# A two-block hybrid decoder: gate and up products token by token with 512 moving columns, product transposed on TensorE, three norms in token halves

## The reference, cut to what matters

```
def swiglu(h, w_gate, w_up, w_down):
    return (jax.nn.silu(h @ w_gate) * (h @ w_up)) @ w_down
...
    for l in range(DEPTH):
        x = x + 0.5 * swiglu(rms_norm(x, ffn1_norm[l]), ffn1_w_gate[l], ffn1_w_up[l], ffn1_w_down[l])
        h = rms_norm(x, mix_norm[l])
        mem_n = rms_norm(mem, mem_norm[l])
...
        x = x + 0.5 * swiglu(rms_norm(x, ffn2_norm[l]), ffn2_w_gate[l], ffn2_w_up[l], ffn2_w_down[l])
```

## Time and profile before

| | us |
|---|---|
| median of 3 runs | 1759.2 |
| the runs | 1759.13 to 1759.99 |
| the profiled execution | 1756.48, its span 1754.7 |

### The profile page before, as it was taken

How to read it: one execution, slowest core, us unless ns; L and a number is a source line. 1 busy time by engine, 2 the same in 40 slices (tenths; PEclk the granted TensorE clock), 3 DMA queues, 4 the chain that set the end, 5 groups by cost and what they waited for, 6 DMA issues and landing times.

```text
span 1754.7 us, 27203 instructions
## 1 busy us (share of the span) xinstructions
PE 1661.3 (95%) x11578; PEld 1531.1 (87%) x11578; DVE 1048.1 (60%) x1506; ACT 872.9 (50%) x1297; POOL 97.7 (6%) x72
## 2 busy tenths in 40 slices
PE   7999899999989899999888999999999998789999
PEld 7989777989977799999887899989999997679998
DVE  6875564896646555555786645455646465555554
ACT  4975363686445435435445533344454357443332
POOL 0112000012200000000240000000000000000000
PEclk9999999999999899999999999998999999899999
DMA  7624224552313465555321555544665553035552
GB/s 224 191 66 135 71 73 145 157 158 89 97 49 117 163 213 191 171 190 169 121 83 62 168 186 179 188 140 135 196 204 175 185 169 120 24 113 179 190 192 97
DMA packets 204297, 253.24 MB, mean 144 GB/s; under 512 B 17808, under 2 KB 183952, under 8 KB 204048
## 3 DMA queue, kind: packets, MB, share of 16 engines
q1 hardware_dynamic: 204176, 251.49, 44.9%
HBM read 250.43 MB, written 1.05 MB: 143 GB/s over the span
## 4 chain that ended last, share of the span: by engine, by line
PE 78%; DVE 8%; ACT 6%; issue 5%; DMA 1%; POOL 1%; SPq 0%; DVEq 0%; ACTq 0%; POOLq 0%
PE bank L784 77%; ACT arena L1377 4%; DVE weights_rest L1889 2%; ACT weights_high L1377 1%; PE bank L842 1%; DVE arena L2036 1%; DMA ring<-in_w_in 1%; ACT L1377 1%; ACT L1372 1%; DVE small L2206 0%; DVE x L2252 0%; DVE weights_rest_more L1889 0%; DVE arena L2224 0%; POOL arena L2520 0%; DMA vec<-in_vec 0%
## 5 line engine op out<-in xcount | busy, mean ns | idle before, releaser
L784 PE MATMUL bank<-xT_high,weights_high 128*128 128x256 f32 (+1 forms) x2352 | 676.1, 288 | 8.9 <-DVE weights_rest L1889 4.1
L784 PE MATMUL bank<-xT_rest,weights_high 128*128 128x256 f32 (+1 forms) x2352 | 658.3, 284 | 0.0
L784 PE MATMUL bank<-xT_high,weights_rest 128*128 128x256 f32 (+1 forms) x2048 | 581.4, 285 | 0.0
L1889 DVE TENSOR_TENSOR weights_rest<-ring,weights_high 128x1024 fp32r<-128x1024 f32 (+3 forms) x414 | 486.6, 1225 | 98.8 <-ACT weights_high L1377 95.1
L1377 ACT ACTIVATE weights_high<-ring 128x1024 fp32r<-128x1024 f32 (+3 forms) x414 | 400.6, 1019 | 253.9 <-PE bank L784 235.6
L784 PEld LDWEIGHTS bank<-xT_high,weights_high 128*128 128x128 f32 (+1 forms) x2352 | 454.2, 193 | 19.4 <-issue 8.9
L784 PEld LDWEIGHTS bank<-xT_rest,weights_high 128*128 128x128 f32 (+1 forms) x2352 | 448.1, 192 | 3.5 <-issue 2.0
L784 PEld LDWEIGHTS bank<-xT_high,weights_rest 128*128 128x128 f32 (+1 forms) x2048 | 395.7, 193 | 0.6
L1377 ACT ACTIVATE arena<-bank 128x512 f32<-128x512 f32 (+4 forms) x253 | 134.5, 547 | 390.3 <-PE bank L784 327.4
L784 PE MATMUL bank<-arena 128*128 128x128 f32 (+2 forms) x1416 | 209.4, 307 | 37.3 <-ACT arena L1377 22.9
L784 PEld LDWEIGHTS bank<-arena 128*128 128x128 f32 (+1 forms) x1416 | 180.2, 203 | 63.6 <-ACT arena L1377 22.6
(11 more groups left out here) (180 smaller groups left out, 1698.1 us busy)
## 6 DMA issues: line engine op xcount, KB each, us to landing
ring<-in_w_in SPq DMA_DIRECT2D x36, 1024.0 KB, 5.2
ring<-in_ffn_w_gate SPq DMA_DIRECT2D x36, 1024.0 KB, 5.4
ring<-in_ffn_w_up SPq DMA_DIRECT2D x35, 1024.0 KB, 5.4
ring<-in_ffn_w_down SPq DMA_DIRECT2D x34, 1024.0 KB, 4.9
ring<-in_w_out SPq DMA_DIRECT2D x22, 1024.0 KB, 4.9
ring<-in_w_in_a SPq DMA_DIRECT2D x11, 1024.0 KB, 5.2
ring_more<-in_ffn_w_down SPq DMA_DIRECT2D x10, 1024.0 KB, 5.1
ring_more<-in_ffn_w_up SPq DMA_DIRECT2D x9, 1024.0 KB, 5.3
```

The lines of the kernel that those rows point to most:

```text
L784: return eng.matmul(o, a, b, start=first, stop=last)
L1889: TTs(rest_slot(b)[:, part], raw_slot(b)[:, part], high_slot(key)[:, part].bitcast(F32), ALU.subtract).then_inc(*dv.mark(("rest", key, z)))
```

## The change

**Gate and up.** A weight block now holds four of the eight 128-row slices of both matrices, 256 gate columns beside 256 up columns. There are two such blocks a pair, (g, j, 0) and (g, j, 1), each landed by two transfers of 512 KB. `gate_up` holds 128 tokens of `xh` or `xl` stationary and moves 512 columns of weights: 48 matmuls of 512 columns a pair. Within a block the slices come in the order 2, 3, 0, 1, so the first matmul asks for both pieces of the block.

**The product** is made token-major in halves of 128 tokens by 256, then four transposes of a pair bring it back (`hidden_transposes`). ScalarE copies the high part out of the bank (`hidden_high`) and VectorE subtracts (`hidden_rest`); VectorE's cast goes.

**The norms** of f10, f20 and f21 run by token halves (`norm_by_tokens`, `add_and_norm`): the first half is added, scaled, transposed and multiplied in pair 0 before the second. `first_block` goes, `st_final` becomes a part of them. The last two down products are interleaved by token halves. ScalarE and VectorE split up to two blocks ahead of pair 0's SiLU, where it was three.

```diff
-                cols((st, "g", j), w[f"{n}_w_gate_2"][l], 256 * j, 256 * j + 256)
-                cols((st, "u", j), w[f"{n}_w_up_2"][l], 256 * j, 256 * j + 256)
+                for z in range(2):
...
+                    out.append(((st, "g", j, z), pieces, (4, 512)))
...
+            def gate_up(st, j, z, t, b, order):
...
+                for n, k in order:
+                    if j == 0 and id in BY_TOKENS.values():
+                        pe.wait_ge(*at(("xl", id, t, k)))
...
+                    if k % 4 >= 2:
+                        second_half(key)
+                    for i, (a, v) in enumerate(products(wv, [xh, xl])):
+                        ins = mm(b[:, 0:512], v[:, k, t * P:t * P + P], a[:, k % 4, :], n == 0 and i == 0, n == KD - 1 and i == 2)
...
+                    if j == 0 and id in BY_TOKENS.values():
+                        for z in range(2):
+                            gate_up(st, j, z, 0, b[0], order[4 * z:4 * z + 4])
+                        transposes(id, 1)
+                        for z in range(2):
+                            gate_up(st, j, z, 1, b[1], order[4 * z:4 * z + 4])
+                    else:
+                        for z in range(2):
+                            for t in range(NT):
+                                gate_up(st, j, z, t, b[t], order[4 * z:4 * z + 4])
+                            if j and z == 0:
+                                hidden_transposes(st, j - 1)
...
+                    if j and j < pairs - 1:
+                        down(st, j - 1, (0, 1), (0, 1), used=True)
+                if end == pairs:
+                    down(st, pairs - 2, (0,), (0, 1))
+                    hidden_transposes(st, pairs - 1)
+                    down(st, pairs - 2, (1,), (0,))
+                    down(st, pairs - 1, (0,), (0, 1))
+                    down(st, pairs - 2, (1,), (1,), used=True)
+                    down(st, pairs - 1, (1,), (0, 1), used=True)
...
                 for j in range(begin, end):
-                    g = (id, "g", j)
-                    split_until(split_no[(st, "g", j)] + 3)
...
+                    split_until(split_no[(st, "g", j, 0)] + (3 if j else 2))
+                    if j:
+                        hidden_high(st, j - 1)
+                    for t in range(NT):
+                        g = (id, "gu", j, t)
+                        copy(sg[:, j % 2, t, :], g, ps(g, 2, S)[:, 0, :], (id, "s", j, t), func=ACT.Silu)
                 if end == PAIRS:
-                    split_until(split_no[(st, "d", PAIRS - 1)] + 3)
+                    n = split_no[(st, "d", PAIRS - 1)] + 1
+                    split_until(n)
+                    hidden_high(st, PAIRS - 1)
+                    split_until(n + 2)
...
+            def add_and_norm(st, id):
...
+                add(0)
+                scale(0)
+                if id == "f20":
+                    split_until(n, more=1)
+                    slices(0, SLICES)
+                    add(1)
+                else:
+                    slices(0, SLICES[:4])
+                    add(1)
+                    split_until(n, more=1)
+                    slices(0, SLICES[4:])
+                split_until(n, more=2)
+                scale(1)
+                slices(1, SLICES)
```

More of the change, by code:

```diff
@@ L647, in two_blocks @@
         SLICES = (2, 3, 0, 1, 4, 5, 6, 7)
+        BY_TOKENS = {"h1": "f10", "s0": "f20", "s1": "f21"}
         def slices_of(st):
@@ L798, in feature_major @@
                 ins.then_inc(*pe.mark(gkey, used=key))
[L800 to L815, removed]
             def token_major(key, gkey, wv, n, K, src):
@@ L834, in st_norm @@
                     eng.wait_ge(sems("ident_in"), 16)
+                if id in BY_TOKENS.values():
+                    transposes(id, 0)
+                    return
                 gs = [k // 2 for k in slices_of(st)[::2]]
-                b = {g: group(("nt", id, g), among=range(4, 8) if id in ("f10", "f20", "f21") else None) for g in sorted(gs)}
+                b = {g: group(("nt", id, g)) for g in sorted(gs)}
                 for t in range(NT):
@@ L1158, in st_pv @@
                 ins.then_inc(*pe.mark(("pv", name, hp)))
[L1160 to L1164, removed]
-                    if k:
[L1166 to L1184, removed]
@@ L1221, in st_ffn @@
                 st = ffn_of(st)
-                need_xT(id)
+                if id in BY_TOKENS.values():
+                    fresh[0] = None
+                else:
+                    need_xT(id)
                 acc_open[0] = True
[L1224 to L1237, removed]
+                order = list(enumerate(SLICES))
@@ L1877, in split_until @@
             def split_until(n, ahead=0, more=0):
-                n = 2 * min(reach((pieces[0] + 1) // 2, n, ahead), len(split)) + more
+                n = 2 * min(reach((pieces[0] + 1) // 2, n, ahead) if ahead else n, len(split)) + more
                 while pieces[0] < n:
@@ new lines, in add_acc, with slices, add @@
+            def add_acc(st, scale):
+                added = [add_half(st, t, scale) for t in range(NT)]
+                for nx in sched[place[st] + 1:]:
+                    if nx[0] == "norm" and nx[2] == "x":
+                        for t in range(NT):
+                            new.at[("x_ready", nx[1], t)] = added[t]
+                        break
+            def add_and_norm(st, id):
+                gain = next(nx[3] for nx in sched if nx[0] == "norm" and nx[1] == id)
+                n = (pieces[0] + 1) // 2 + 1
+                split_until(n)
+                def slices(t, ks):
+                    for k in ks:
+                        v = ps(("nt", id, t, k // 2), 2, P)
+                        src, g = v[:, k % 2, :], V(gain)[:, k:k + 1]
+                        to = slice(t * P, t * P + P)
+                        if k == 2:
+                            dv.wait_ge(*at(("nt", id, t, 1)))
+                            for q in (2, 3):
+                                TS(xh[:, q, to], v[:, q % 2, :], V(gain)[:, q:q + 1], None, ALU.mult).then_inc(*dv.mark())
+                            dv.wait_ge(*dv.last())
+                        if k not in (2, 3):
+                            dv.wait_ge(*at(("xh", id, t, k)))
+                            dv.wait_ge(*at(("xh", id, t, k ^ 1)))
+                        STT(out=xl[:, k, to], in0=src, scalar=g, in1=xh[:, k, to].bitcast(F32), op0=ALU.mult,
+                            op1=ALU.subtract).then_inc(*dv.mark(("xl", id, t, k), frees=("nt", id, t, k // 2)))
+                def add(t):
+                    new.at[("x_ready", id, t)] = add_half(st, t, 1.0)
+                    if id == "f10":
```

200 lines of the change are left out of this document (127 added, 73 removed).

## The result

The changed kernel takes 1777.8 us (median of 4 runs, 1776.8 to 1781.4), the kernel before beside it 1759.2 us (1757.9 to 1760.0): ratio 1.0119, 95% interval 1.0092 to 1.0147. It is slower, by 18.6 us; forecast were 23.5. Taken again beside other runs of the kernel before, the ratio was 1.0141 (1.0112 to 1.0170), 25.8 us between the medians. The forecast lies between the two. The median of the kernel before was 1759.2, 1755.1, 1752.4 and 1754.7 us in the four sets of runs, so times are compared within a set. In the experiment with the third block, two of 12 runs took 6290 and 9183 us at full granted clock, for a reason that nothing recorded shows, and they are left out there.

The account below looks back on a forecast made before the run. TensorE, busy 95% of the span, was taken as the bound, with its waits at the norms. Terms -5.7 + 16.8 + 7.3 - 3.5 + 2.6 + 6.0 = +23.5 on 1759.2 gave 1782.7 us, range 1757 to 1799.

Parts of the forecast that it names:

- The pair stream: Every pair on TensorE: 48 matmuls at 0.228 us plus four transposes, gain 0.13 a pair, -5.7 us for 44 pairs.
- The fast rival: Wide matmuls in the pair stream are cheap, distance falling towards 0.213 us: 1753 us in all; chance 0.11.
- the slow bound: 512-column matmuls in the pair stream at twice the 256-column price, 0.240 us: 26 us more.
- The second rival: No change: pair 0's halves overlap, norms give 12 us more, no lower clock, cheaper stream: 1759 us; chance 0.08.
- the six named waits: New TensorE idle times of 3.65 to 4.2 us: pair 1 in four networks, pair 5 in f10 and f11.
- the third rival: Some 36 pairs each wait for late splits, 0.5 us each, 18 us more, 1801 us; chance 0.09.
- Pair 0 to pair 1: Pair 1's first block is split behind ScalarE's SiLU; TensorE waits 4.2 us in each of four networks, +16.8 us.
- The memory norm's front: In f10 and f11 ScalarE's table load, squares and roots delay pair 5's first block: 3.65 us twice, +7.3.
- The norms by halves: Norms of f10, f20 and f21 by token halves: -3.5, +0.6 and -0.6 us after the stream's share, together -3.5.
- The sign of being wrong: In f10, pair 0 ending before 610 would show the prediction wrong; 613.5 was forecast.
- The small ones: f11's start +0.4, each network's end 0.3 late (+1.2), the end of f20 +1.0: together +2.6 us.
- The clock: Lower clock behind four of six new waits, 1.5 us each: +6.0 us, between 0 and 10.

Follow-up runs that it names:

- the experiment with the third block: Changed kernel with ScalarE and VectorE splitting three blocks, not two, ahead of the SiLUs in pair 0: 1756.2 us, 1.0006 of the kernel before.
- the two runs with ScalarE alone changed: Blocks split in pair 0: kernel before with ScalarE at two, VectorE at three, 0.9991; changed kernel with ScalarE at three, VectorE at two, 1.0139.
- the first two experiments: Changed kernel with three blocks split in pair 0, 1756.2 us; changed kernel with pair 5's first block split ahead of the memory norm's front, 1770.6 us.
- the two with new waits of 3.1 and 3.3 us: Kernel before with two blocks split in pair 0 on both engines, 1780.2 us; changed kernel with ScalarE at three, VectorE at two, 1778.8 us.
- waits of 2.24 to 2.68: Changed kernel with TensorE taking the input slices in the order 0, 1, 2, 3 from pair 1 on: 1770.8 us, 1.0087 of the kernel before.

## Why the prediction was right, point by point

**The pair stream.** 0.228 was taken for 512 columns, and 0.227 was measured, in one bank as between banks. The four transposes cost 0.35 up to the next matmul and 0.10 in those behind it, 0.45 together, as forecast (0.44). A pair gained 0.19 us, not 0.13, since 72 matmuls of 512 columns, those of the down product too, cost a little less than 0.228: 44 x 0.19 = 8.4 us instead of 5.7. The fast rival (0.213) did not come, nor the slow bound. The second rival (waits half as long, norms 12 us better) did not come either. A plain pair took 16.79, and behind pair 0 the six named waits are the only ones for a weight block, so the third rival (every pair waits) is out too.

**Pair 0 to pair 1.** Forecast: TensorE goes on 4.2 us after its last matmul. Measured: 610.25 to 614.54, less the 0.23 of the matmul itself, 4.06, and 3.90 of idle time in all four networks. 16.2 us instead of 16.8. The experiments bear out the place and the price. The prediction named ScalarE's SiLU as what holds the block up; the two runs with ScalarE alone changed show that VectorE's product in front of the subtraction does so as well. It said that before, "the gate block of pair 1 was split ahead of the SiLU", but not that this was by the number three and not by the form of the product. The number alone brings 3.10 us of wait into the kernel before.

**The memory norm's front.** Forecast 3.65 twice, measured 3.38 of idle time, some 3.5 of path: 7.0 instead of 7.3.

**The norms by halves.** From the end of the output product to the end of pair 0 (the wait's row less its idle time):

- f10: 593.90 to 617.9 before, 24.0; 591.20 to 610.64 after, 19.4: 4.5 less (unrounded), forecast 4.1. The sign of being wrong, an end before 610, was nearly reached, but the stage itself began 2.7 us sooner, in matmuls that the change leaves alone.
- f20: 17.0 before; 18.7 after in a profile with 3.4 us of low clock inside, 17.2 in the second one with none. Forecast: no difference.
- f21: 18.3 before, 16.8 after: 1.5 less, forecast 1.2.

Taking away what the stream has already, about 4.1 instead of 3.5. The profile shows why it is little in f20: in place of one wait of 3.27 us TensorE has 1.84 ahead of the first half's transposes, 1.46 ahead of its first matmul and 0.43 ahead of the second half's.

**The small ones.** The end of f20 was put at +1.0 for a wait of 4.3 us ahead of the transposes. It did not come; the idle time is 3.28, as in the earlier trace rows:

```profile
1183.88 1.51 PE L843 MATMUL bank<-const,arena 128*128 128x128 f32 x6 [3.28 <-DVE arena L2012]
```

The other 1.6 lie below what the stages can show; no run tests them, and the sum below keeps them as forecast.

**The clock.** The mechanism was right, the size too small. Forecast were four of six waits with 1.5 us each, 6.0. All six had the lower clock behind them, two for over 6 us, and keeping TensorE busy gave 8.3 us back. That is 1.4 a wait: as far as the runs can tell, the price was right and the count wrong, taken from two of three waits in one profile. That profile has a fourth such wait, which the prediction passed over: 3.27 us ahead of f21's transposes, up to 1560.53, with the lower clock from 1561.1 to 1564.5. That two of the stretches were 6.8 us long does not show in the price; the uncertainty of the 8.3 is larger than that.

**The sum with what was measured:** -8.4 + 16.2 + 7.0 - 4.1 + 1.6 + 8.3 = +20.6, between the 18.6 and the 25.8 of the two comparisons. The forecast of +23.5 was right in sign and size; its errors, 2.7 and 0.6 too little gain from the stream and the norms, 1.0 too much for f20's end, 0.9 too much for the waits and 2.3 too little for the clock, cancel in part. That the total fits so well is in some measure luck. By stages the forecast says +5.2 for f10, +4.7 for f20, +10.1 up to the end of f11 and +3.5 for f21; the two profiles say 6.6 and 5.8, 7.6 and 5.1, 9.9 and 12.7, 3.3 and 3.3.

## What to carry to other kernels

When two in-order engines prepare the operand of a third, look at both queues for what stands in front of that preparation, and at the place where the usual cover (here the down product) is not there yet: the first step and the step with extra work. A cheaper inner loop of 0.2 us in 17 is soon eaten by a few waits of 4 us, so price the waits first. And price a wait of 3 to 4 us on a full TensorE at more than itself: here by about a third again (some 8.3 us on 22.4 us of waits), for the lower clock behind it.

## What was not expected of the hardware

- The granted clock was at its lower level behind six of six waits of 3.4 to 3.9 us in the changed kernel's profile, and again in its second. Over the profiles of six runs (these two, the first two experiments and the two with new waits of 3.1 and 3.3 us) it was so behind 27 of 28 waits of 3.1 to 3.9 us ahead of pairs 1 and 5. The one without is f20's, 3.29 us, with three blocks on ScalarE and two on VectorE. With waits of 2.24 to 2.68 it fell at three of the same six places, and with 28 transposes of a constant in the wait and 0.33 to 0.85 us of idle time left, at none. Here small transposes whose result nobody reads held the clock up, and they saved some 8.3 us. Three of the places with 2.68 or 2.24, the first and third rows at full clock:

```profile
616.60:619.90 3.30, 3.30 (x14) 2.72 (x15) 3.30 (x4) 3.30 (x4) 0.00 (x0) 1.00 0.73 241
686.60:690.00 3.40, 3.40 (x11) 2.64 (x11) 3.40 (x4) 3.13 (x4) 0.00 (x0) 0.62 0.72 248
999.10:1002.40 3.30, 3.30 (x15) 2.73 (x16) 3.30 (x4) 3.30 (x4) 0.00 (x0) 1.00 0.70 232
```

- A 512-column matmul with a weight load of its own takes 0.227 us whether the bank changes or stays, and 48 of them cost 0.6 us less than 96 of 256 columns.
